# Gate, output projection, norm and first GEMM of the second block as one program by token tiles

## The chip, the cores and the metric

The kernel runs on one core of one Trainium2 chip. The metric is the device time of one execution in microseconds, as the median over runs. Engines are called as in the profile: PE (TensorE), DVE (VectorE), ACT (ScalarE), POOL (GpSimd) and SP (SyncE, which here only issues transfers).

## The reference, cut to what matters

Two transformer blocks follow each other on 1024 tokens of width 1024, all in float32. The piece around the change:

```python
        o_diff = rms_norm(o_diff, diff_subln_g[layer]) * (1.0 - lam_init)
        o_diff = o_diff.transpose(0, 2, 1, 3).reshape(B, T, DIFF_WIDTH) * jax.nn.silu(dz)
        ...
        o_nsa = o_nsa.transpose(0, 3, 1, 2, 4).reshape(B, T, NSA_WIDTH) * jax.nn.silu(nz)
        x = x + jnp.concatenate([o_diff, o_nsa], axis=-1) @ w_out[layer]
    return x
...
        h = rmsnorm(x, norm_mix_pre[i])
        proj = h @ w_in[i]
        z, xbc, dt_raw, q, k, v = jnp.split(proj, IN_OFFSETS, axis=-1)
```

The norm of `o_diff` is over each head's 128 columns, that of x over all 1024.

## The kernel before

The kernel is a row of stages, each a block of five engine programs that ends with a barrier and orders itself by semaphores that are written out by hand. Nothing schedules it: on each engine the order is that of the code. Tokens are tiled by 128 (`NT` = 8 tiles), the contraction by 128 (`KT` = 8 steps).

A product keeps float32 accuracy by splitting: ACT copies an operand into the rounded format fp32r (the high part), DVE subtracts it from the original (the low part), and PE adds up high x high, low x high and high x low, three matmuls for one. So each 128x512 tile of weights costs ACT a copy and DVE a subtraction, and so does each half of a transposed tile of activations.

Between the last attention stage of the first block ("di") and the windowed attention of the second ("w2") there were five stages:

- "mt", `transposed_stage` with the `prep` of line 1379. DVE squares and sums the heads of all eight tiles, ACT takes all roots at once, then DVE builds tile after tile: norm, gain `subln`, gate z (loaded back from DRAM by SP), the NSA half. PE transposes a tile in eight pieces of 128x128, ACT and DVE write its high and low part into `mT`.
- "o1", `gemm_stage` with two jobs of 512 columns. k is the outer loop, and all eight token tiles' banks are open; a ring of three weight tiles is split by ACT and DVE. DVE adds x (loaded into `xr`) in each bank at the end of a job; POOL issues the loads of x and the stores of x1.
- `end_part` (line 2990): SP clears all semaphores used so far.
- `params2_stage` (line 1430): small parameters and masks of the second block; ACT's Exp on `nA` waits for all of them.
- "n2", `norm_transposed` (line 1204): ACT squares all eight tiles of x1 with a sum along the row, one root, one reciprocal; then DVE scales a row and PE transposes it, into `h2T`.
- "g2", `gemm_stage` with four jobs: two of 512 columns of Q, one of K (each key column twice), one of 288 columns of V and dt. Q and K are column jobs (weights stationary, banks of 128 columns x 512 tokens), V is a row job. POOL builds the tables of the window attention meanwhile (`window2_tables`).

The last stage, `mix_mlp_stage` (line 2365), is written in another way, with class `Weights` (line 2195): every weight tile has a place of its own (`slot`) that is filled as soon as a named job has released it, and up to eight loads are on the way. Its output projection runs tile by tile: `mix_product(c, t)` adds the 24 matmuls of one token tile and one half of the columns into one bank, and the transpositions of a later tile stand between two products. Four banks hold products and four hold transpositions.

## Time and profile before

| | us |
|---|---|
| median of 3 runs | 3121.11 |
| lowest and highest | 3121.0, 3122.52 |
| the profiled execution's own time | 3118.35 |
| its span | 3116.6 |
| PE busy | 2692.8 |
| DVE busy | 1454.6 |
| ACT busy | 1022.3 |
| POOL busy | 236.0 |

The span runs from the first to the last instruction of the profiled execution; what lies between it and the execution's own time is its start and end. Busy times of engines overlap, so they don't add up to the span. The mean granted clock of PE is 0.923 of full speed (2.4 GHz); a stretch that shows 0.50 ran at the lower of its two levels.

### The profile page before, as it was taken

How to read it: one execution, taken by the hardware profiler on the slowest of the kernel's cores; microseconds unless marked ns; L12 is line 12 of the kernel's file. 1: busy time of each engine (PE TensorE's matmuls, PEld its weight loads, DVE VectorE, ACT ScalarE, POOL GpSimd, SP SyncE). 2: the span in 40 equal slices, each digit the busy share in tenths (PEclk: the TensorE clock that was granted, in tenths of full speed). 3: DMA queues.
4: the chain of work that ended last, by engine and by line, in shares of the span. 5: the costliest groups of instructions: out<-in, count | busy, mean ns of one | idle time of the engine just before them, and what ended most of it. 6: DMA issues, size and time to landing. Idle time of an engine off the chain costs nothing. (4 is left out here: it accounts for less than half of the span.)

```text
span 3116.6 us, 35479 instructions
## 1 busy us (share of the span) xinstructions
PE 2692.8 (86%) x13168; PEld 2186.9 (70%) x13168; DVE 1454.6 (47%) x3307; ACT 1022.3 (33%) x2250; POOL 236.0 (8%) x240
## 2 busy tenths in 40 slices
PE   3999966799966758498998998989869999999998
PEld 2888855677955646387666887567457888888877
DVE  3111157756788862313882212556776322322234
ACT  3112233344664410313882113245134212222132
POOL 1000002000020000200110000023600000000000
PEclk8999976698988969699999999979989999999999
DMA  2112210000000032110003112100044111111113
GB/s 88 49 48 76 65 56 1 1 1 1 1 1 1 1 138 78 39 48 19 23 24 114 48 64 82 54 1 1 1 172 146 41 55 48 48 48 48 51 48 139
DMA packets 102651, 153.10 MB, mean 49 GB/s; under 512 B 35024, under 2 KB 49488, under 8 KB 102480
## 3 DMA queue, kind: packets, MB, share of 16 engines
q1 hardware_dynamic: 95312, 125.67, 13.0%
q0 software_dynamic: 4864, 16.78, 1.4%
q10 hardware_dynamic: 2304, 8.39, 0.7%
q8 instruction: 105, 1.72, 0.2%
q14 instruction: 66, 0.54, 0.1%
HBM read 121.44 MB, written 29.36 MB: 48 GB/s over the span
## 5 line engine op out<-in xcount | busy, mean ns | idle before, releaser
L2280 PE MATMUL banks<-mhT,mmwhi 128*128 128x512 f32 x1024 | 316.2, 390 | 3.9 <-ACT qsq L2589 2.8
L2271 PE MATMUL banks<-mmwhi,fT 128*128 128x512 f32 x1024 | 315.8, 390 | 3.7 <-ACT qsq L2589 3.7
L381 PE MATMUL banks<-g1whi,hT 128*128 128x512 f32 (+1 forms) x1024 | 301.7, 378 | 5.7 <-DVE g1wlo L347 5.7
L2256 DVE TENSOR_TENSOR mmwlo<-mmwraw,mmwhi 128x512 fp32r<-128x512 f32 x144 | 97.2, 689 | 369.3 <-ACT mmwhi L2252 369.3
L2252 ACT ACTIVATE mmwhi<-mmwraw 128x512 fp32r<-128x512 f32 x144 | 89.3, 629 | 413.5 <-DMA mmwraw<-in_w_down 207.4
L2271 PEld LDWEIGHTS banks<-mmwhi,fT 128*128 128x128 f32 x1024 | 191.8, 188 | 45.3 <-ACT qsq L2589 5.5
L2280 PEld LDWEIGHTS banks<-mhT,mmwhi 128*128 128x128 f32 x1024 | 191.6, 188 | 45.5 <-ACT qsq L2589 4.1
L381 PEld LDWEIGHTS banks<-g1whi,hT 128*128 128x128 f32 x1024 | 189.2, 189 | 41.3 <-DVE g1wlo L347 6.1
L2271 PE MATMUL banks<-mmwlo,fT 128*128 128x512 f32 x512 | 199.3, 389 | 0.0
L2280 PE MATMUL banks<-mhT,mmwlo 128*128 128x512 f32 x512 | 199.3, 389 | 0.0
L381 PE MATMUL banks<-g1wlo,hT 128*128 128x512 f32 (+1 forms) x512 | 193.4, 378 | 0.0
L347 DVE TENSOR_TENSOR g1wlo<-g1raw,g1whi 128x512 fp32r<-128x512 f32 (+1 forms) x64 | 42.4, 662 | 261.2 <-ACT g1whi L324 261.1
L381 PE MATMUL banks<-h2T,g3whi 128*128 128x512 f32 x384 | 119.7, 393 | 7.5 <-DVE g3wlo L347 7.5
L381 PE MATMUL banks<-h2T,g2whi 128*128 128x512 f32 x384 | 119.8, 393 | 5.8 <-DVE g2wlo L347 5.8
L324 ACT ACTIVATE g1whi<-g1raw 128x512 fp32r<-128x512 f32 (+1 forms) x64 | 38.9, 607 | 251.4 <-PE banks L381 246.7
L2271 PEld LDWEIGHTS banks<-mmwlo,fT 128*128 128x128 f32 x512 | 96.1, 188 | 20.1
L2280 PEld LDWEIGHTS banks<-mhT,mmwlo 128*128 128x128 f32 x512 | 96.1, 188 | 19.9
L381 PEld LDWEIGHTS banks<-g1wlo,hT 128*128 128x128 f32 x512 | 96.5, 189 | 17.5
L347 DVE TENSOR_TENSOR g3wlo<-g3raw,g3whi 128x512 fp32r<-128x512 f32 x40 | 27.6, 692 | 169.8 <-ACT g3whi L324 169.6
L2104 ACT ACTIVATE sdE<-banks,vnA 128x128 f32<-128x128 f32 x256 | 69.9, 376 | 74.0 <-PE banks L2050 74.0
L1667 PE MATMUL banks<-w2pt,v 128*128 128x512 f32 x176 | 92.3, 609 | 0.0
L2089 DVE TENSOR_TENSOR sdE<-sdE,CBT 128x512 f32<-128x512 f32 x64 | 69.5, 1104 | 48.3 <-ACT sdE L2104 48.3
(451 smaller groups left out, 5788.3 us busy)
## 6 DMA issues: line engine op xcount, KB each, us to landing
mmwraw<-in_w_up SPq DMA_DIRECT2D x64, 256.0 KB, 2.7
mmwraw<-in_w_down SPq DMA_DIRECT2D x64, 256.0 KB, 2.6
g1raw<-in_w_in SPq DMA_DIRECT2D x56, 256.0 KB, 2.6
g3raw<-in_w_in SPq DMA_DIRECT2D x40, 256.0 KB, 2.6
qx<-x_scratch SPq DMA_DIRECT2D x16, 512.0 KB, 6.5
xt<-in_x SPq DMA_DIRECT2D x8, 512.0 KB, 6.5
z_scratch<-zst POOLq DMA_DIRECT2D x16, 256.0 KB, 2.6
cw<-in_cmp_w SPq DMA_DIRECT2D x2, 2048.0 KB, 9.3
```

Source lines behind the costliest of these rows:

```text
L324: nc.scalar.activation(whi[n % RING][:, w_slice(n)], raw[n % RAW][:, w_slice(n)], ACT.Copy).then_inc(hi_ready, 1)
L347: nc.vector.tensor_tensor(wlo[n % RING][:, w_slice(n)], raw[n % RAW][:, w_slice(n)], f32(whi[n % RING][:, w_slice(n)]), ALU.subtract).then ...
L381: last = nc.tensor.matmul(out, l, r, start=(k == 0 and i == 0), stop=(k == job.nk - 1 and i == 2))
L1667: nc.tensor.matmul(psum[6 + w % 2][:, :], v2[:, k, w % G // 2 * 2 * HD:(w % G // 2 + 1) * 2 * HD], pt[c % PT][:].rearrange("p h q -> p (h ...
L2089: nc.vector.tensor_tensor(E[u % 4][:], E[u % 4][:], CBT[:, c, g:g + 1, :].to_broadcast([P, 4, P]), ALU.mult).then_inc(g_ready, 1)
L2104: nc.scalar.activation(E[u % 4][:, i, :], psum[u % 4][:, i * P:(i + 1) * P], ACT.Exp, bias=V["nA"][:, d, c, 4 * q + i:4 * q + i + 1]).then ...
L2252: self.nc.scalar.activation(self.hi[n][:], self.raw[n][:], ACT.Copy).then_inc(self.hi_ready, 1)
L2256: self.nc.vector.tensor_tensor(self.lo[n][:], self.raw[n][:], f32(self.hi[n][:]), ALU.subtract)\
L2271: ins = self.nc.tensor.matmul(out, l, r[:], start=k == 0 and i == 0, stop=k == self.nk[j] - 1 and i == 2)
L2280: ins = self.nc.tensor.matmul(out, l[:, col], r, start=k == 0 and i == 0, stop=k == self.nk[j] - 1 and i == 2)
```

## The change

The five stages from the gate to the first GEMM become one block, `mix1_qkv_stage`. Class `Weights` moves up in the file and learns weight tiles of less than 512 columns and tiles that come in two loads. What is new or in another place:

- DVE's norm of the heads goes tile by tile: ACT squares a tile's 512 columns into the row buffer, DVE sums, ACT takes four roots per row, and one DVE operation per head multiplies norm and gate. The gain `subln` is multiplied into the z tile by POOL.
- The output projection runs tile by tile in two passes (first the left half of the columns for all tiles, then the right). The transpositions of tile t + 2 stand behind the product of tile t in the first pass. x1 overwrites `o_diff` and `o_nsa`.
- The norm of x1 is in two parts: ACT squares and sums the left half between the passes, the right half as it comes, and the root takes the left half's sum as its bias. Stores of x1 are issued by ACT in half tiles. The rows of tile t - 2 are transposed behind the product of tile t in the second pass, those of tiles 6 and 7 between the first products of V.
- V and dt come first of the second block's jobs, tile by tile, then Q in two jobs and K.
- The parameters of the second block are loaded and its masks built inside this block; the semaphores of the earlier stages are cleared by SP during the attention stage.
- K's low part, V and the tables get other places in memory.

```diff
+    old = list(used)
+    def clear_old(sp, o_done):
+        for s in old:
+            sp.sem_clear(s)
+    attention_stage(nc, sem, "di", mem, C, units, 2, psum2, psum, 41, 73, 81, store=clear_old)
...
+    first_slots = [153 + 4 * i for i in range(KT)]
+    second_slots = [4 * i for i in range(6)] + [41, 45]
+    for c in range(2):
+        w.job(NT, [(wo[k * P:(k + 1) * P, half_cols(c)], (first_slots if c == 0 else second_slots)[k], None)
+                   for k in range(KT)])
...
+    JV = w.job(NT, [(v_and_dt(k), first_slots[k], w.release(0, k)) for k in range(KT)], 256 + H2)
+    JQ = [w.job(8, [(s, second_slots[k], w.release(1, k)) if k < 7 else (s, first_slots[0], w.release(JV, 0))
+                    for k, s in enumerate(columns(C_Q))])]
...
+                if i >= XR:
+                    sp.wait_ge(mixed, i - XR + 1)
...
+            load_z(0)
+            load_z(1)
+            for n in w.steps(0):
+                w.load(sp, n)
+            sp.dma_start(C["gain"][:], a["norm_mix_pre_2"][0].partition_broadcast(P)).then_inc(g_in, 16)
+            for i in range(XR):
+                load_x(i)
+            for t in range(2, NT):
+                load_z(t)
+                w.load(sp, KT + t - 2)
+            w.load(sp, KT + 6)
+            w.load(sp, KT + 7)
+            for i in range(XR, NT):
...
+            for n in w.steps(JV):
+                w.load(sp, n)
+            for i in range(NT, 2 * NT):
+                load_x(i)
...
+            for j in (JQ[0], JQ[1], JK):
+                for n in w.steps(j):
+                    w.load(sp, n)
...
+            for t in range(NT):
+                pool.wait_ge(z_in[t % 2], 16 * (t // 2 + 1))
+                nc.gpsimd.tensor_tensor(zt[t % 2][:, 0:512].rearrange("p (h d) -> p h d", h=4),
+                                        zt[t % 2][:, 0:512].rearrange("p (h d) -> p h d", h=4),
+                                        C["subln"][:].unsqueeze(1).to_broadcast([P, 4, P]), ALU.mult).then_inc(zs, 1)
+            pool.wait_ge(zs, NT)
+            pool.wait_ge(mixed, 2 * NT)
+            pool.wait_ge(small_in, 16 * 10)
+            T["build"](pool, C["sink"][:])
+            pool.wait_ge(t2, 2 * NT)
...
+                if t >= 2:
+                    act.wait_ge(t1, 2 * (t - 1))
+                nc.scalar.activation(row[t % 2][:, 0:512], o_diff[:, t, :], ACT.Square).then_inc(o_sq, 1)
...
+            def norm_root(t):
+                act.wait_ge(mixed, NT + t + 1)
+                nc.scalar.activation(zj[t % 2], x1[1][:, t, :], ACT.Square, accum_out=st[:, t, 10:11]).then_inc(b_sq, 1)
+                act.wait_ge(b_sq, t + 1)
+                act.wait_ge(a_bias, t + 1)
+                nc.scalar.activation(st[:, t, 11:12], st[:, t, 10:11], ACT.Sqrt, scale=1.0 / DM, bias=st[:, t, 9:10])\
+                    .then_inc(x_root, 1)
+                store(1, t)
...
+            head_squares(0)
+            head_roots(0)
+            head_squares(1)
+            for n in range(2):
+                w.high(act, n)
+            high(0, t1, hi1)
+            for n in range(2, KT):
+                w.high(act, n)
+            head_roots(1)
+            for t in range(NT):
+                if t + 2 < NT:
+                    head_squares(t + 2)
+                if t >= 1:
+                    high(t, t1, hi1)
+                if t + 2 < NT:
+                    head_roots(t + 2)
+                w.high(act, KT + t)
...
+            for t in range(NT):
+                if t >= 2:
+                    act.wait_ge(b_sq, t - 1)
+                norm_root(t)
+                if t >= 2:
+                    high(t - 2, t2, hi2)
+                w.high(act, w.first[JV] + t)
+            for t in range(NT - 2, NT):
+                high(t, t2, hi2)
...
+            for t in range(NT):
+                if t < 7:
+                    w.high(act, w.first[JQ[0]] + t)
+                v_rows(t)
...
+            def rows(t):
+                dve.wait_ge(o_root, t + 1)
+                nc.vector.reciprocal(st[:, t, 4:8], st[:, t, 4:8]).then_inc(o_rec, 1)
+                dve.wait_ge(o_rec, t + 1)
+                dve.wait_ge(zs, t + 1)
+                for h in range(4):
+                    d = tile(h)
+                    nc.vector.scalar_tensor_tensor(out=row[t % 2][:, d], in0=o_diff[:, t, d], scalar=st[:, t, 4 + h:5 + h],
+                                                   in1=zt[t % 2][:, d], op0=ALU.mult, op1=ALU.mult).then_inc(r_done, 1)
+                nc.vector.tensor_tensor(row[t % 2][:, 512:1024], o_nsa[:, t, :], zt[t % 2][:, 512:1024], ALU.mult)\
+                    .then_inc(r_done, 1)
...
+            head_sums(0)
+            rows(0)
+            head_sums(1)
+            for n in range(2):
+                w.low(dve, n)
+            low(0, hi1, lo1)
+            rows(1)
+            for n in range(2, KT):
+                w.low(dve, n)
+            for t in range(NT):
+                if t + 2 < NT:
+                    head_sums(t + 2)
+                if t >= 1:
+                    low(t, hi1, lo1)
+                if t + 2 < NT:
+                    rows(t + 2)
+                w.low(dve, KT + t)
+                if t >= 1:
+                    mix(0, t - 1)
+            mix(0, NT - 1)
+            for t in range(NT):
+                mix(1, t)
+                bias(t)
+                if t >= 2:
+                    low(t - 2, hi2, lo2)
+                x_rows(t)
+                w.low(dve, w.first[JV] + t)
...
+            def mix_product(c, t):
+                if c == 0:
+                    pe.wait_ge(lo1, 2 * (t + 1))
+                if NT * c + t >= 4:
+                    pe.wait_ge(mixed, NT * c + t - 3)
+                for k in range(KT):
+                    if t == 0:
+                        pe.wait_ge(w.lo_ready, KT * c + k + 1)
+                    w.rows(c, k, hT, k, tile(t), psum[t % 4][:], t == NT - 1)
...
+            def v_product(t):
+                pe.wait_ge(lo2, 2 * (t + 1))
+                if t < 4:
+                    pe.wait_ge(mixed, NT + 5 + t)
...
+                    pe.wait_ge(v_done, t - 3)
+                for k in range(KT):
+                    if t == 0:
+                        pe.wait_ge(w.lo_ready, w.first[JV] + k + 1)
+                    w.rows(JV, k, hT, k, tile(t), psum[t % 4][:, 0:256 + H2], t == NT - 1)
...
+            t1_rows(0)
+            t1_rows(1)
+            for t in range(NT):
+                mix_product(0, t)
+                if t + 2 < NT:
+                    t1_rows(t + 2)
+            for t in range(NT):
+                mix_product(1, t)
+                if t >= 2:
+                    t2_rows(t - 2)
+            v_product(0)
+            v_product(1)
+            t2_rows(6)
+            v_product(2)
+            v_product(3)
+            t2_rows(7)
+            for t in range(4, NT):
+                v_product(t)
...
-    transposed_stage(nc, sem, "mt", C["ident"], DM, mT[0], mT[1], rowbuf, prep, psum, load=load_z, act_prep=act_prep)
...
-    gemm_stage(nc, sem, "o1", mem, 153, [out_job(0), out_job(1)], psum, pool_jobs=store_x1)
...
-            sp.wait_ge(x1_out, 16 * NT)
...
-    norm_transposed(nc, sem, "n2", mem, C, lambda t: x1[:, t, :], hT[0], hT[1], psum, 57, None, none)
...
-    gemm_stage(nc, sem, "g2", mem, 153,
...
-        end_part(nc, used)
```

`w.high(act, n)` is ACT's copy of weight tile n and `w.low(dve, n)` DVE's subtraction; `high` and `low` are the same for a transposed tile. `release(j, k)` is the point at which job j has used its weight tile k for the last time.

PE where the projection begins. Before, all transpositions ("mrow" is the row buffer) stand ahead, then a barrier (the branches), and the first matmuls take one weight tile through different token tiles:

```order
L209 MATMUL banks<-ident,mrow_11579 128x128 x8
L209 MATMUL banks<-ident,mrow_11578 128x128 x8
L209 MATMUL banks<-ident,mrow_11579 128x128 x8
L171 UNCONDITIONAL_BRANCH
L353 UNCONDITIONAL_BRANCH
L381 MATMUL banks<-o1whi_138_11883,mT_11574 128x512
L381 MATMUL banks<-o1whi_138_11883,mT_11575 128x512
L381 MATMUL banks<-o1wlo_141_11886,mT_11574 128x512
L381 MATMUL banks<-o1whi_138_11883,mT_11574 128x512
L381 MATMUL banks<-o1whi_138_11883,mT_11575 128x512
```

In the change, two tiles are transposed ("prow"), and then the first token tile goes through the weight tiles ("pjwhi", "pjwlo"):

```order
L1828 UNCONDITIONAL_BRANCH
L1833 MATMUL banks<-ident,prow_11760 128x128 x8
L1833 MATMUL banks<-ident,prow_11761 128x128 x8
L1317 MATMUL banks<-pjwhi_11712,h2T_11697 128x512
L1317 MATMUL banks<-pjwhi_11712,h2T_11698 128x512
L1317 MATMUL banks<-pjwlo_11711,h2T_11697 128x512
L1317 MATMUL banks<-pjwhi_11715,h2T_11697 128x512
L1317 MATMUL banks<-pjwhi_11715,h2T_11698 128x512
L1317 MATMUL banks<-pjwlo_11714,h2T_11697 128x512
L1317 MATMUL banks<-pjwhi_11718,h2T_11697 128x512
```

The transpositions of the later tiles have moved behind the products of earlier ones.

DVE for one tile of the gate. Before ("mT" is the transposed activation, two halves):

```order
L1393 TENSOR_TENSOR msq_11580<-o_diff_9879,mstat_11582 128x512
L1394 TENSOR_TENSOR msq_11580<-msq_11580,subln 128x512
L1396 TENSOR_TENSOR mrow_11579<-msq_11580,zt_11577 128x512
L1398 TENSOR_TENSOR mrow_11579<-o_nsa_3922,zt_11577 128x512
L1401 COPY mstat_11582<-mstat_11582 128x1
L186 TENSOR_TENSOR mT_11575<-banks,mT_11574 128x4x128 x2
```

In the change, for the first pass's fifth round ("pjwlo" is a weight tile's low part, L1752 the residual):

```order
L1727 TENSOR_REDUCE pstat_11765<-prow_11760 128x4
L1745 TENSOR_TENSOR h2T_11698<-banks,h2T_11697 128x4x128 x2
L1732 RECIPROCAL pstat_11765<-pstat_11765 128x4
L1737 SCALAR_TENSOR_TENSOR prow_11760<-o_diff_9879,pstat_11765,pz_11758 128x128 x4
L1739 TENSOR_TENSOR prow_11760<-o_nsa_3922,pz_11758 128x512
L1301 TENSOR_TENSOR pjwlo_11747<-pjwraw_11746,pjwhi_11748 128x512
L1752 TENSOR_TENSOR o_diff_9879<-banks,pxt_11762 128x512
```

The gain's product has left DVE, and a weight tile and a residual of the projection have come between two tiles' rows.

ACT where the second block's first products end. In the change the copies of the last two transposed tiles ("h2T", four halves) stand ahead of the first evacuation of V ("v", "dt_raw"), with the split of Q's first weight tile between them:

```order
L1637 DMA x_scratch<-o_nsa_3922 128x512
L1633 ACTIVATE h2T_11697<-banks 128x4x128 x2
L1296 ACTIVATE pjwhi_11733<-pjwraw_11731 128x288
L1633 ACTIVATE h2T_11697<-banks 128x4x128 x4
L1296 ACTIVATE pjwhi_11736<-pjwraw_11734 128x512
L1690 ACTIVATE v_129_11701<-banks 128x256
L1692 ACTIVATE dt_raw_11703<-banks 128x32
L1296 ACTIVATE pjwhi_11739<-pjwraw_11737 128x512
```

Before, V's evacuation was the last work of its stage, and no copy of an activation stood near it.

## Rows read from the trace of the kernel before

**Rows 1.** The page: busy time (share) x instructions; then a group of matmuls with its idle time.
```profile
PE 2692.8 (86%) x13168; PEld 2186.9 (70%) x13168; DVE 1454.6 (47%) x3307; ACT 1022.3 (33%) x2250; POOL 236.0 (8%) x240
...
L381 PE MATMUL banks<-h2T,g2whi 128*128 128x512 f32 x384 | 119.8, 393 | 5.8 <-DVE g2wlo L347 5.8
```

**Rows 2.** Stretches: us, busy us (instructions) of PE, PEld, DVE, ACT, POOL, granted clock, DMA share, GB/s.
```profile
1094.30:1144.60 50.30, 15.79 (x65) 12.59 (x65) 43.81 (x74) 12.08 (x20) 3.52 (x7) 0.54 0.30 98
1144.60:1149.30 4.70, 4.70 (x11) 3.73 (x12) 0.72 (x2) 0.98 (x2) 0.80 (x2) 0.50 0.99 371
1149.30:1234.20 84.90, 84.86 (x374) 69.88 (x373) 19.17 (x29) 8.22 (x13) 3.05 (x6) 1.00 0.23 83
1234.20:1302.30 68.10, 14.14 (x64) 11.51 (x64) 22.85 (x33) 22.99 (x38) 12.74 (x34) 0.55 0.26 67
1302.30:1306.30 4.00, 3.99 (x9) 3.14 (x10) 1.55 (x2) 0.63 (x1) 3.62 (x5) 0.50 0.65 190
1306.30:1434.70 128.40, 128.40 (x568) 106.31 (x567) 24.71 (x36) 23.54 (x38) 1.64 (x4) 1.00 0.18 43
1434.70:1460.30 25.60, 25.60 (x194) 25.35 (x192) 4.55 (x9) 6.00 (x19) 0.00 (x0) 1.00 0.08 19
```

**Rows 3.** Groups of instructions, 1094 to 1142 us: busy us, mean ns | idle before it, releaser.
```profile
L209 PE MATMUL banks<-ident,mrow 128*128 128x128 f32 x64 | 15.8, 428 | 29.3 <-DVE mstat L1401 29.3
...
L1384 DVE TENSOR_REDUCE mstat<-msq 128x4 f32<-128x512 f32 x8 | 5.5, 686 | 0.3
```

**Rows 4.** Timeline, 1252 to 1463 us: start us, length us, engine, line, operation [idle before, releaser].
```profile
1252.14 0.33 SPq L1453 DMA_DIRECT2D gain<-in_norm_mix_pre  x1
...
1263.23 0.23 ACT L1489 ACTIVATE nA<-nA 128x32 f32<-128x32 f32 x1 [9.80 <-DMA convb<-in_conv_b]
...
1278.05 3.67 PE L209 MATMUL banks<-ident,n2rb 128*128 128x128 f32 x16 [43.89 <-DVE n2rb L1227]
...
1462.03 1.06 ACT L1694 ACTIVATE w2qs<-q2T 64x1024 fp32r<-64x1024 f32 x1 [0.28 <-PEq L291]
```

**Rows 5.** Timeline of the last stage's start (the last row is a stretch, as in rows 2).
```profile
2274.62 0.32 SPq L2459 DMA_DIRECT2D qz<-z_scratch  x1
...
2277.80 1.22 DVE L2630 TENSOR_TENSOR y<-y,qz 128x1024 f32<-128x1024 f32 x1 [3.46 <-DMA qz<-z_scratch]
...
2296.78 1.97 PE L2772 MATMUL banks<-ident,y 128*128 128x128 f32 x8 [10.51 <-DVE y L2625]
2298.40 1.20 PE L2271 MATMUL banks<-mmwhi,mhT 128*128 128x512 f32 x2
...
2304.55 1.04 PE L2772 MATMUL banks<-ident,y 128*128 128x128 f32 x8
...
2317.23 1.04 PE L2772 MATMUL banks<-ident,y 128*128 128x128 f32 x8
...
2274.60:2298.40 23.80, 3.59 (x17) 3.20 (x17) 14.27 (x20) 12.11 (x22) 0.00 (x0) 0.52 0.92 338
```

**Rows 6.** Groups of instructions of the whole span, one engine each.
```profile
L1161 DVE SCALAR_TENSOR_TENSOR dix<-dix,dist,dix 128x512 f32<-128x512 f32 x4 | 3.0, 751 | 0.1
L1161 DVE SCALAR_TENSOR_TENSOR dix<-dix,dist,dix 128x128 f32<-128x128 f32 x4 | 1.4, 350 | 0.1
L324 ACT ACTIVATE o1whi<-o1raw 128x512 fp32r<-128x512 f32 x16 | 10.1, 632 | 68.9 <-PE banks L381 61.1 <-DMA o1raw<-in_w_out 7.8
L2926 ACT ACTIVATE v<-banks 128x256 f32<-128x256 f32 x8 | 3.0, 379 | 6.2 <-PE banks L381 6.2
L609 POOL TENSOR_TENSOR hntmp<-nq,hnrstd 128x512 f32<-128x512 f32 x8 | 10.1, 1258 | 69.7 <-DVE hnrstd L624 62.5 <-DVE hnst L632 7.2
```

**Rows 7.** Timeline, 1475 to 1483 us, POOL and DVE.
```profile
1475.39 2.35 POOL L1735 TENSOR_TENSOR w2qs<-q2T,w2qs 64x1024 fp32r<-64x1024 f32 x1 [167.15 <-ACT w2qs L1694]
1475.65 2.11 DVE L1767 TENSOR_TENSOR w2sk<-w2low,wnsink 128x4 f32<-128x4 f32 x1
...
1482.48 0.16 DVE L1767 TENSOR_TENSOR w2sk<-w2low,wnsink 128x4 f32<-128x4 f32 x1
```

More of the change, by code:

```diff
@@ L1233, in silu_store, with tile, half_cols @@
+def tile(t):
+    return slice(t * P, (t + 1) * P)
+def half_cols(c):
+    return slice(c * 512, (c + 1) * 512)
 def silu_store(nc, name, sem, stage, jobs_z, scratch, table_of):
@@ L1254, in silu_store, with first_block @@
     return take, pool_jobs
-def first_block(nc, sem, mem, a, C, S, big, x1_dram, scr_z):
+def first_block(nc, sem, mem, a, C, S, big, scr_z, used):
     psum = [big[:, 512 * i:512 * (i + 1)] for i in range(8)]
@@ L1356, in first_block @@
                               o_diff[:, t, h * P:(h + 1) * P], False))
-    attention_stage(nc, sem, "di", mem, C, units, 2, psum2, psum, 41, 73, 81)
-    mT = [mem.at("mT", 89 + 32 * i, [P, KT, SEQ], F32R) for i in range(2)]
-    zt = [mem.at("zt", 8 * i, [P, DM], F32) for i in range(2)]
-    rowbuf = [mem.at("mrow", 73 + 4 * i, [P, DM], F32) for i in range(2)]
-    sq = [mem.at("msq", 81 + 2 * i, [P, 4, P], F32) for i in range(2)]
-    stat = mem.at("mstat", 85, [P, 2, NT * 4], F32)
-    z_in = [sem(f"z_in{i}") for i in range(2)]
@@ L1417, in store_x1 @@
-    def store_x1(pool, act_out, dve_out, table):
-        for t in range(NT):
-            pool.dma_start(xr[:, t, :], x[t * P:(t + 1) * P, :]).then_inc(xr_in, 16)
-        for t in range(NT):
-            pool.wait_ge(dve_out, NT + t + 1)
-            pool.dma_start(x1_dram[t * P:(t + 1) * P, :], xr[:, t, :]).then_inc(x1_out, 16)
-    gemm_stage(nc, sem, "o1", mem, 153, [out_job(0), out_job(1)], psum, pool_jobs=store_x1)
-    S["x1_out"] = x1_out
-    return xr
-def params2_stage(nc, sem, mem, a, C, x1_out):
+    old = list(used)
@@ L1432, in params2_stage, with params2_layout @@
+def params2_layout(mem, C):
     mem.const_at = mem.kept
@@ L2284, in tile @@
-def tile(t):
-    return slice(t * P, (t + 1) * P)
-def half_cols(c):
-    return slice(c * 512, (c + 1) * 512)
 def attn_part_stage(nc, sem, mem, wo, ya, y_in, part_dram, psum, a_kb, w_kb, part_kb, part_out):
@@ L2868, in _, with second_block @@
                             w.rows(j, k, fT[k // 4], k % 4, tile(t), psum[t][:], t == NT - 1)
-def second_block(nc, sem, mem, a, C, S, big, x1, x1_dram, scr_z, scr_yT, part_dram, x2_dram, out, used):
+def second_block(nc, sem, mem, a, C, S, big, o_diff, o_nsa, x1_dram, scr_z, scr_yT, part_dram, x2_dram, out, used):
     psum = [big[:, 512 * i:512 * (i + 1)] for i in range(8)]
-    params2_stage(nc, sem, mem, a, C, S["x1_out"])
+    params2_layout(mem, C)
     hT = [mem.at("h2T", 89 + 32 * i, [P, KT, SEQ], F32R) for i in range(2)]
-    none = lambda eng, t: None
-    norm_transposed(nc, sem, "n2", mem, C, lambda t: x1[:, t, :], hT[0], hT[1], psum, 57, None, none)
@@ L2879, in second_block @@
     w = a["w_in_2"][0]
     qT = mem.at("q2T", 0, [P, ATT_HEADS // 2, SEQ], F32)
-    kT = [mem.at("k2T", 32 + 16 * i, [P, ATT_KV, SEQ], F32R) for i in range(2)]
-    v2 = mem.at("v2", 64, [P, NT, ATT_KV * HD], F32)
+    k_hi = mem.at("k2T", 32, [P, ATT_KV, SEQ], F32R)
+    v2 = mem.at("v2", 48, [P, NT, ATT_KV * HD], F32)
+    k_lo = mem.at("k2T", 56, [P, ATT_KV, SEQ], F32R)
     dt_raw = mem.at("dt_raw", 88, [P, NT, 2 * SSM_HEADS], F32)
-    T = window2_tables(nc, sem, mem, 183, 183.75, 171)
-    qscale = T["qscale"]
@@ L3017, in build @@
         params1_stage(nc, sem, mem, a, C)
-        x1 = first_block(nc, sem, mem, a, C, S, big, x1_dram, scr_z)
-        end_part(nc, used)
-        second_block(nc, sem, mem, a, C, S, big, x1, x1_dram, scr_z, scr_yT, part_dram, x2_dram, out, used)
+        o_diff, o_nsa = first_block(nc, sem, mem, a, C, S, big, scr_z, used)
+        second_block(nc, sem, mem, a, C, S, big, o_diff, o_nsa, x1_dram, scr_z, scr_yT, part_dram, x2_dram, out, used)
 _INS = ["x", "norm_g", "w_in", "diff_q_norm_g", "diff_k_norm_g", "diff_lambda_q1", "diff_lambda_k1",
```

503 lines of the change are left out of this document (314 added, 189 removed).

## The prediction

> **What bounds the kernel now.** I read the page first: TensorE (PE) is busy 86% of the span, VectorE (DVE) 47%, ScalarE (ACT) 33% [rows 1]. So PE is the bound and the changed part is worth what PE waits in it, not what its other engines do. The table of stretches splits that part by PE's state [rows 2]. The last attention value is evacuated at 1094.3 us; then come 50.3 us in which PE is busy 15.8 (64 transpositions at a granted clock of 0.54), the output projection (4.7 us at half clock, 84.9 at full), 68.1 us in which PE is busy 14.1, and the first GEMM of the second block (4.0 us at half clock, 128.4 at full for Q and K, 25.6 for V and dt). From 1094.3 to 1460.3 that is 366.0 us.
>
> The two holes have plain causes. In the first, DVE is busy 43.8 of 50.3 us: it squares and sums all eight tiles before ACT takes the roots, then builds the rows tile by tile, with PE waiting 29.3 us for it [rows 2, 3]. In the second, small loads and semaphore clearing come first: no engine computes from 1235 to 1252.1, the Exp on nA waits 9.8 us for the last parameter, then ACT squares eight tiles before the first row exists; PE waits 43.9 us in one piece [rows 4]. Inside the first GEMM of the second block PE waits for nothing but the first weights, 5.8 us [rows 1], and its products fill the projection's stretch just as tightly [rows 2]. So there is room to win only in the holes and the two warm-ups.
>
> **The sum, part by part.** The new program uses the pattern that the kernel has already in its last stage (gate, transposition, output projection by token tiles), so most prices can be read there.
>
> *Products.* Their number is unchanged. Q and K are 576 matmuls in 132.4 us; half of the 4.0 us at half clock is lost, so 130.4 us is the full-clock cost, 0.226 each. The projection's 384 give 89.6 - 2.4 = 87.2 us. V is 25.6 [rows 2]. Together 243.2 us. The order changes from k outside to tile outside, so 24 matmuls in a row add into one bank. In the last stage a tile done that way takes 5.44 us (2298.40 to 2304.55 is 6.15 with the warm-up, and the next two repeat every 6.34 with transpositions) [rows 5]: 24 x 0.227, no charge.
>
> *Transpositions.* Of 16 groups of eight, 14 now stand between products. A group with its neighbours' switching costs 6.34 - 5.44 = 0.9 us at full clock [rows 5], against 1.97 at half clock in the holes [rows 5]. 14 x 0.9 = 12.6 us on the path.
>
> *The start.* From 1094.6: z of tile 0 lands after 3.2 us (2274.62 to 2277.80) [rows 5]; the new GpSimd (POOL) product of z with subln takes 1.26 like a 128x512 product in the first block [rows 6], to 4.5. Square, sum (0.6 + 0.69), a table load and the root of tile 0 are ready before that. DVE's row is four products of 128x128 at 0.35 and one of 128x512 at 0.69, as long as a sum [rows 3, 6], to 6.6; transposition 2.0, to 8.6. Tile 1 comes next, but its root stands on ACT behind the splitting of six weight tiles, and these behind z0, z1 and the weights before them on one queue: 3 MB. At the 338 GB/s of the last stage's start [rows 5] that is 9 us and some 3 of latency, so the root is there at about 13, the row at 15.2, and the first product 1.6 us after its transposition begins [rows 5]: 17.2 us after 1094.3 with the stage's change. The lower bound is 13 (weights early). The upper is 23.8, which the last stage took from its first load to its first product [rows 5]; there one more load of 512 KB stands before the weights, and the whole z tile is gated on DVE ahead of the second row. So I take 17.2. Warm-up: the last stage lost 0.7 us in its first tile, the projection 2.4; I take 1.2.
>
> *First pass.* PE needs 6.34 per tile. DVE has, per tile, a sum, two low parts, a weight's low part and the residual, which are five operations of 128x512 at 0.69 or a little less, and a row of 2.1 + 0.2: 5.6 [rows 3, 6]. As a chain from the end of one transposition (ACT's square 0.6 first) that is 6.2 to 6.3, just inside PE's period; PE needs the low parts 3.7 us later than they come. Charge 0.
>
> *Second pass and V.* DVE's chain after tile 7 is residual 0.7, ACT's square, root and store issue, its two copies, DVE's low parts, two scaled rows of 0.75 each [rows 6], then the low part of V's last weight tile: about 6.2 us after the product's end. V's first tile reaches that weight at 0.9 + 7 x 0.4 = 3.7. Wait 2.5. POOL begins its table work then, see below; 3.0 with it. Second wait: ACT copies hT for tiles 6 and 7 before it evacuates any V tile, and tile 7's transposition stands behind V tile 3. V tile 4 needs bank 0 back, which comes 1.2 us of copies, 0.63 of a weight and the evacuation (0.38 and a smaller one) after the transposition, counted with the copy that overlaps it: 2.1 [rows 6]. Bounds 0 and 8 for the two waits together. Q and K start without a wait: their weights are loaded under V.
>
> *Small loads, constants, masks, x1 stores.* Under 200 us of products; on SyncE's queue the parameters stand before Q's weight loads, which are due some 30 us later, and ACT issues 16 stores between its squares. Charge 0. If that cover were gone, it is the 18 us before 1252.1 and the 11 after it [rows 4]. The block change itself (semaphores cleared) moves under 140 us of attention.
>
> *Tail.* K ends the program now instead of V: the last bank's copy 0.6 and low part 0.69 against V's shorter evacuation; but that runs behind today, and the next stage starts 1.7 us after PE ends at 1460.3 [rows 4]. Equal.
>
> Sum: 17.2 + 1.2 + 243.2 + 12.6 + 5.1 = 279.3 against 366.0: 86.7 us less. The profiled execution's own time is 3118.35 (span 3116.6 and 1.75 around it), so 3031.7 by it. The median of the runs is 3121.11, 2.8 above; I forecast the median of runs: **3034**.
>
> **GpSimd beside VectorE.** The rows show a price that the sum leaves out. While POOL multiplies for 2.35 us, a DVE product of 128x4 takes 2.11 us and ends with it; alone it takes 0.16 [rows 7]. The new pass has a POOL product of 1.26 per tile, and DVE's row products and weight low parts read two SBUF operands. Eight times 1.26 is 10 us if all of it fell on PE's path. By the chain it falls at 1.7 to 3.0 us after the transposition, under the low parts, which read one operand from PSUM (whether these wait too, no row shows), and PE has 3.7 us of slack; so I charge 0.5 at V only.
> The Trainium skill (SBUF — State Buffer, section "SBUF: two separate sides") says why: the two engines share one port pair, taken as a lock for a whole instruction. By that rule the sum would be between +0 and +10 us; this trace agrees that the wait is the whole rest of POOL's instruction.
>
> **Rivals.**
> 1. *DVE's chain paces the first pass.* For: 6.2 to 6.3 of 6.34 us leaves nothing, and locks of up to 1.26 come on top. Against: in the last stage DVE gates a whole tile (1.22 [rows 5]), scales it, and does the same low parts and residual, and PE keeps 6.34. With 7.5 per tile over 7 to 12 tiles: +8 to +14, 3042 to 3048. It needs PE's slack of 3.7 to be used up first.
> 2. *Loads hold the start.* As in the last stage, 23.8 instead of 17.2: 3041.
> 3. *Half clock through both passes, slower than before.* In the first hole PE worked half of the time, in bursts of transpositions, and the granted clock stayed at its lower level (1.2 of 2.4 GHz): mean 0.54 there, 0.55 in the second [rows 2]. If the tile program made PE pause in every tile, by a late row or a late bank, the clock could stay there: 384 products and 14 groups cost 87 + 13 more, plus the pauses, 3134 and up. It decides from about 14 of 16 tiles at the lower level, since the gain is 86.7 and a tile costs 6.3. Against it: 6.34 us per tile in the last stage is the full clock.
> The Trainium skill (TensorE: Matmul & The Clock Gate, section "HAM oscillation — how this bites in real kernels") tells of a kernel that fell back in every K tile because it waited for a load there; here by that rule only tiles with a wait would pay, and the last stage's rows show none.
> 4. *The change doesn't bring its overlap*, because a queue order serialises one pass (SyncE holds the x tiles behind z tile 7 and 16 loads of V): one hole of about 40 us comes back, 3075.
>
> **How the numbers follow.** Forecast 0.72 (3025 to 3041, with starts of 13 to 20 and waits of 0 to 8); rival 1 0.12; rival 2 0.10; rival 4 0.04; rival 3 0.02. The range of 3024 to 3048 holds the forecast and rivals 1 and 2 and leaves less than 2 in 10 outside. What a measurement can tell from no change here is about 0.2%, 6 us. Faster 0.975, within 0.015 (a mix of rivals 3 and 4), slower 0.01.
>
> **What would show it.** Right: about 17 us from the end of the attention to the first product; transposition groups every 6.3 us in both passes at clock 1.00; one wait of 2 to 3 us at V's first tile for a weight's low part, one near V's fifth tile for ACT; no wait at Q. Wrong: a wait at each product of the first pass (rival 1), loads as releasers before 1112 (rival 2), matmuls of over 0.6 us after the first tile (rival 3), or a hole of tens of us between the passes (rival 4).

## The result and the profile after

| | before | changed |
|---|---|---|
| median of the runs, us | 3121.06 (4 runs) | 3031.32 (4 runs) |
| lowest and highest | 3119.87, 3122.52 | 3026.34, 3039.78 |
| the profiled execution's own time | 3118.35 | 3032.81 |
| its span | 3116.6 | 3031.1 |

The changed kernel takes 0.9715 of the time before (95% interval 0.9692 to 0.9738): 89.7 us less by the medians, 85.5 by the profiled executions. Forecast were 3034 and 86.7 less by the profiled execution. A second comparison of the same two kernels gave 3030.49 and 0.9717 (0.9700 to 0.9735).

The page, as in [rows 1] (the second row is the group with V's first tile in it):

```profile
PE 2680.7 (88%) x13168; PEld 2179.8 (72%) x13168; DVE 1444.6 (48%) x3325; ACT 1024.3 (34%) x2286; POOL 247.0 (8%) x236
...
L1317 PE MATMUL banks<-pjwhi,h2T 128*128 128x512 f32 (+1 forms) x384 | 108.2, 368 | 4.7 <-DVE pjwlo L1301 2.5
```

PE is busy 12 us less and the span is 85.5 shorter. In the stretches between the end of the attention and the end of the GEMM alone PE was busy 277.5 of 366.0 us [rows 2] and is now busy 263.0 of 283.2: its idle time fell by 68.3, and the same matmuls take 14.5 less, since fewer run at the lower clock. The stretches, with the columns of [rows 2]: the start, the first tile, the two passes, V and dt, then Q and K.

```profile
1092.90:1111.95 19.05, 3.59 (x17) 3.19 (x17) 10.29 (x21) 8.95 (x16) 4.84 (x3) 0.63 0.79 281
1111.95:1119.00 7.05, 7.05 (x28) 5.71 (x27) 6.58 (x14) 2.31 (x5) 4.34 (x2) 0.79 0.29 103
1119.00:1211.90 92.90, 92.53 (x457) 77.36 (x456) 57.88 (x117) 33.95 (x82) 6.56 (x4) 1.00 0.50 146
1211.90:1245.40 33.50, 29.13 (x212) 28.69 (x211) 12.48 (x19) 11.86 (x31) 20.64 (x41) 0.95 0.12 40
1245.40:1376.10 130.70, 130.70 (x578) 107.91 (x576) 21.20 (x31) 21.66 (x36) 0.30 (x1) 1.00 0.12 32
```

The first hole of [rows 2] is now 19.05 us long, and in the place of the second stands nothing, since V follows the second pass in the same microsecond. In the 92.9 us of the passes PE waits once, for 0.4 us. All waits of PE in the stage (waited for: us in total, times, longest):

```profile
PE banks L1833 <- DVE prow L1739: 15.9, 2, 9.9
PE banks L1317 <- DVE pjwlo L1301: 2.5, 1, 2.5
PE banks L1317 <- ACT dt_raw L1692: 1.8, 1, 1.8
PE banks L1317 <- DVE h2T L1745: 0.4, 1, 0.4
```

The start in the timeline (start us, length us, engine, line, operation [idle before, releaser]):

```profile
1093.15 0.82 SPq L1544 DMA_DIRECT2D pz<-z_scratch  x2
...
1098.32 2.48 POOL L1587 TENSOR_TENSOR pz<-pz,subln 128x512 f32<-128x512 f32 x2 [157.12 <-DMA pz<-z_scratch]
...
1099.68 2.05 DVE L1737 SCALAR_TENSOR_TENSOR prow<-o_diff,pstat,pz 128x128 f32<-128x128 f32 x4 [4.06 <-POOL pz L1587]
...
1104.89 3.21 ACT L1296 ACTIVATE pjwhi<-pjwraw 128x512 fp32r<-128x512 f32 x6
1108.00 0.28 ACT L1627 ACTIVATE pstat<-pstat,eps 128x4 f32<-128x4 f32 x1
...
1108.53 1.14 DVE L1737 SCALAR_TENSOR_TENSOR prow<-o_diff,pstat,pz 128x128 f32<-128x128 f32 x4
...
1110.33 1.97 PE L1833 MATMUL banks<-ident,prow 128*128 128x128 f32 x8 [5.97 <-DVE prow L1739]
```

The loads of z were issued from 1093.15 on, and GpSimd began its product for tile 0 at 1098.32. The four row products of tile 0 took 2.05 us beside GpSimd's work on tile 1, those of tile 1 took 1.14. ScalarE copied six weight tiles (3.21 us) before tile 1's root at 1108.00, and PE waited 5.97 for the row that hangs on that root.

**How far the runs lie apart.** The changed kernel's four runs lie 13.4 us apart, those of before 2.7 here and up to 11.5 in later comparisons. To compare stages I therefore use three marks of each trace: the end of the last attention value's evacuation, the first product of the projection, and the end of the GEMM's last matmul (K's in the changed kernel, V's before). A time with a plus sign is counted from the first mark. The stage between the first and the last mark took 283.25 us in the changed kernel (366.0 before), and 281.69 in the second profile.

### The profile page after: what moved, and what is told of

The parts are those of the page before. It is cut to its first block and busy times, and to the rows that moved or that the text cites. A ratio compares the mean times of both kernels' runs of the same rounds, so it can differ in the third digit from the quotient of the medians.

```text
span 3031.1 us, 35487 instructions
## 1 busy us (share of the span) xinstructions
PE 2680.7 (88%) x13168; PEld 2179.8 (72%) x13168; DVE 1444.6 (48%) x3325; ACT 1024.3 (34%) x2286; POOL 247.0 (8%) x236
## 5 line engine op out<-in xcount | busy, mean ns | idle before, releaser
L1326 PE MATMUL banks<-h2T,pjwhi 128*128 128x512 f32 x384 | 118.3, 389 | 0.0
L1317 PE MATMUL banks<-pjwhi,h2T 128*128 128x512 f32 (+1 forms) x384 | 108.2, 368 | 4.7 <-DVE pjwlo L1301 2.5
```

The costliest lines, as they stand in the source:

```text
L1317: ins = self.nc.tensor.matmul(out, l, r[:, c], start=k == 0 and i == 0, stop=k == self.nk[j] - 1 and i == 2)
L1326: ins = self.nc.tensor.matmul(out, l[:, col], r, start=k == 0 and i == 0, stop=k == self.nk[j] - 1 and i == 2)
```

## The experiments

**The same kernel again.**

> The changed kernel as it is, in five rounds beside the kernel before, to see how far its runs lie apart. Its four runs so far lie between 3026.3 and 3039.8, those of before between 3119.9 and 3122.5. If the spread belongs to the new stage, the stretch from the end of the attention to the last matmul of K (283.2 us in the first profile) moves by several us from one profile to the next; if it belongs to the rest of the kernel, that stretch stays within 1 us and other stretches move. Median 3031, ratio 0.9715.

Median 3030.49 (3025.4 to 3036.6). The stage moved by 1.6 us, 1.5 of it in V (33.46 and 31.97 from V's first product to Q's first), a little more than the 1 us that I had set as the sign. What moved more is far away, in the diagonal part of the scan (the stage that writes `sdE`): 143.9 us in the first profile, 147.6 in this one, 140.8 in the order experiment below. The stretch in this profile, and in that of the order experiment:

```profile
1974.80:2122.40 147.60, 141.35 (x827) 118.27 (x827) 80.69 (x95) 70.23 (x256) 48.32 (x24) 0.85 0.00 1
```

```profile
1977.30:2118.10 140.80, 133.85 (x827) 112.06 (x827) 81.29 (x95) 69.81 (x256) 48.36 (x24) 0.90 0.00 1
```

The same 827 matmuls under a granted clock of 0.85 and of 0.90: 6.8 us between two executions in a stage that the change does not touch. So small edits are read from the stage's own marks, and only their sum from the medians.

**One part of the change alone, in the kernel before.** Clearing of semaphores, small loads and masks:

```diff
-    attention_stage(nc, sem, "di", mem, C, units, 2, psum2, psum, 41, 73, 81)
+    attention_stage(nc, sem, "di", mem, C, units, 2, psum2, psum, 41, 73, 81, store=clear_old)
...
-    gemm_stage(nc, sem, "o1", mem, 153, [out_job(0), out_job(1)], psum, pool_jobs=store_x1)
+    gemm_stage(nc, sem, "o1", mem, 153, [out_job(0), out_job(1)], psum, pool_jobs=store_x1, load_more=small_loads)
...
-        end_part(nc, used)
```

> The kernel before with one part of the change alone: the semaphores are cleared by SyncE during the attention, the eleven small loads are issued and the masks built under the output projection, and what is left between projection and norm is the Exp and four small VectorE operations. My theory: this part is worth what no engine computes in between, 18 us, and most of the 11 us up to the first squares of the norm, less a barrier and the wait for the last stores that stay: 22 to 28 us, so 3093 to 3099. The other 58 to 63 us of the change need the program by token tiles. The rival (most of the gain is the tidying between the stages): 50 us or more, 3070 or less.

Median 3094.54, ratio 0.9921 (0.9906 to 0.9936): 24 us less than the kernel before in the same comparison (median 3118.93), inside the 22 to 28 that I expected. The stage's marks say 17.5 (348.5 against 366.0), which is less than that: the rest lies outside the marks, where in the profiles the attention ended 4.9 us earlier and what follows took 3.5 less. The hole before the norm went from 68.1 to 50.4:

```profile
1231.00:1239.00 8.00, 0.00 (x0) 0.00 (x0) 0.00 (x0) 0.00 (x0) 0.00 (x0) 0.62 0.79 317
1239.00:1242.50 3.50, 0.00 (x0) 0.00 (x0) 1.64 (x4) 1.51 (x2) 0.00 (x0) 0.50 0.01 2
1242.50:1254.00 11.50, 0.00 (x0) 0.00 (x0) 0.41 (x2) 10.77 (x18) 0.00 (x0) 0.50 0.00 1
1254.00:1273.00 19.00, 13.16 (x64) 10.97 (x64) 18.02 (x23) 8.88 (x16) 0.00 (x0) 0.65 0.00 0
```

The 8 us without a computing engine that are left are stores of x1 (317 GB/s) behind the projection's end. They are in the kernel before too, where the DMA share is 1.02 up to 1239 us, 0.73 in the next 4 us and 0 behind them; I had put all 18 us down to clearing and small loads. So tidying is worth a fifth of the gain, and the rival that it is most of it falls.

**The overlap of the first pass taken back.** All tiles of the gate are transposed first:

```diff
-            t1_rows(0)
-            t1_rows(1)
+            for t in range(NT):
+                t1_rows(t)
             for t in range(NT):
                 mix_product(0, t)
-                if t + 2 < NT:
-                    t1_rows(t + 2)
...
                 w.low(dve, KT + t)
-                if t >= 1:
-                    mix(0, t - 1)
-            mix(0, NT - 1)
+            for t in range(NT):
+                mix(0, t)
```

> The changed kernel with all eight tiles of the gate transposed ahead of the first product; everything else stays. My theory: VectorE needs some 5 us per tile there (sum 0.67, row 2.0 to 2.9, low parts 1.3, a weight's low part 0.6), so the first product comes 6 x 5 = 30 us later, 6 x 0.9 us of groups no longer stand between products, and warm-up costs about 1 more: +25, so 3056 (3051 to 3061), with a granted clock near 0.5 through the transpositions. The rival (the overlap is worth little, since the time of the first hole went by the cheaper row and the missing barrier): less than +8, under 3040.

Median 3054.95, ratio 0.9793 (0.9776 to 0.9809), stage 307.52: +24.3. The first product comes 47.85 us after the attention's end, nearly the 50.3 of before. The last three of the six transpositions behind the first two, and the stretch:

```profile
1129.22 1.97 PE L1832 MATMUL banks<-ident,prow 128*128 128x128 f32 x8 [2.29 <-DVE prow L1739]
1133.47 1.97 PE L1832 MATMUL banks<-ident,prow 128*128 128x128 f32 x8 [2.28 <-DVE prow L1739]
1137.73 1.97 PE L1832 MATMUL banks<-ident,prow 128*128 128x128 f32 x8 [2.29 <-DVE prow L1739]
...
1110.30:1139.35 29.05, 12.10 (x52) 9.70 (x51) 28.42 (x64) 14.76 (x31) 14.37 (x6) 0.50 0.46 152
```

VectorE is busy 28.42 of 29.05 us and gives a row every 4.25 us (5 expected; the first of the six took 7.5). PE waits 2.3 us for each of the last five, at half clock. So the cheaper row and the missing barrier alone are worth 2.5 us of the first hole; the overlap takes it from 47.85 to 19.08.

**The overlap of the second pass taken back.** Squares and sums stay in the pass; only rows and transpositions go behind it:

```diff
             for t in range(NT):
                 mix_product(1, t)
-                if t >= 2:
-                    t2_rows(t - 2)
+            for t in range(NT):
+                t2_rows(t)
```

> The changed kernel with the rows of x1 transposed behind the whole second pass instead of between its products; squares and sums stay where they are. My theory: per tile 2 x 0.75 for the scaled row and 1.3 for the low parts on VectorE, 3.2 us with the small ones, eight tiles 26 us and 2.5 ahead of them, a warm-up of 1.5; the 7 us of groups inside the products and the two waits of 2.5 and 1.8 us in V go: +18, so 3049 (3044 to 3054). The rival (half clock follows into V and Q): V at half clock adds 20 us more, 3065 and up.

Median 3044.76, ratio 0.9765 (0.9747 to 0.9783), stage 297.39: +14.1. From the last product (1207.43) to V's first (1232.46) it takes 25.0 us; a row came every 2.72 us, not 3.2. V's first 4 us ran at a granted clock of 0.52 and the other 23 at 1.00, so it had a warm-up, and the rival (half clock through V and Q) falls. With the experiment on the small loads this splits the second hole of before: 68.1 to 50.4 by tidying, and 50.4 to 25.0 by what this variant keeps, which are x1's stores, the sums of squares and the weight splitting under the pass and one barrier less. The last 25.0 go by transposing between products, which is worth 14.1 net, as the groups and the two waits of V then stand in the products. Together the three experiments account for 17.5 + 24.3 + 14.1 = 55.9 of the stage's 82.8 us; the other 26.9 were not taken back by themselves, so how they divide is not shown.

**GpSimd beside VectorE.** More products of 128x256 into a spare place behind each product with subln, two and then five per tile:

```diff
+                for _ in range(5):
+                    p_spare.link(nc.gpsimd.tensor_tensor(spare[:], C["subln"][:].unsqueeze(1).to_broadcast([P, 2, P]),
+                                                         C["subln"][:].unsqueeze(1).to_broadcast([P, 2, P]), ALU.mult))
```

> The changed kernel with two more GpSimd products of 128x256 into a spare place behind each product of z with subln, so GpSimd's work beside the first pass is about doubled (16 more instructions of some 0.6 to 0.75 us). My theory: VectorE's operations that read two SBUF operands wait for the rest of a GpSimd instruction (its four row products took 2.05 us beside one and 1.14 without), but PE has slack of some 3.7 us per tile: the groups of transpositions stay 6.34 to 6.36 us apart from the third on, the first product comes at most 1 us later, and the stage from the first transposition to the last matmul (272 to 273 us) grows by 0 to 2. The rival (VectorE's chain is just inside PE's period, so each lock is paid): 0.7 to 1.3 us more per tile over six tiles, +5 to +8.

> The same with five more GpSimd products per tile, so GpSimd works some 5 of 6.3 us. My theory: each of the six SBUF operations that VectorE has per tile waits for most of a GpSimd instruction, 6 x 0.4 to 0.7, which makes a tile's chain 8.5 to 10 us; PE pauses 2 to 3.5 us in each tile of the first pass, and the first pass grows by 12 to 21. It also tries what I called half clock through a pass: with such pauses, do the matmuls stay at 0.39 us or go to 0.63, and does the granted clock of the first pass fall to 0.5 (then +35 and more) or stay near 1? I expect it to stay over 0.8. If VectorE does not wait for GpSimd at all, nothing moves (+0 to +1).

With two, the passes took 100.20 us from the first product to V (99.97 without), so my reading holds there; the start took 2.2 us more, where I had allowed 1. With five the start took 2.5 more and the passes 104.60: +4.6, not 12 to 21. (The single runs took 3031.76 and 3038.55.) VectorE's groups from 1125 to 1160 us, first of the changed kernel, then with five:

```profile
L1737 DVE SCALAR_TENSOR_TENSOR prow<-o_diff,pstat,pz 128x128 f32<-128x128 f32 x16 | 7.7, 541 | 0.1
L1745 DVE TENSOR_TENSOR h2T<-banks,h2T 128x512 fp32r<-128x512 f32 x11 | 7.1, 678 | 0.4 <-ACT h2T L1633 0.4
L1752 DVE TENSOR_TENSOR o_diff<-banks,pxt 128x512 f32<-128x512 f32 x6 | 4.1, 685 | 7.2 <-PE banks L1317 5.0 <-DMA pxt<-in_x 2.1
L1301 DVE TENSOR_TENSOR pjwlo<-pjwraw,pjwhi 128x512 fp32r<-128x512 f32 x6 | 4.1, 680 | 0.0
```

```profile
L1743 DVE SCALAR_TENSOR_TENSOR prow<-o_diff,pstat,pz 128x128 f32<-128x128 f32 x20 | 12.1, 664 | 0.2
L1751 DVE TENSOR_TENSOR h2T<-banks,h2T 128x512 fp32r<-128x512 f32 x12 | 7.6, 675 | 0.0
L1301 DVE TENSOR_TENSOR pjwlo<-pjwraw,pjwhi 128x512 fp32r<-128x512 f32 x6 | 5.3, 888 | 0.0
L1758 DVE TENSOR_TENSOR o_diff<-banks,pxt 128x512 f32<-128x512 f32 x6 | 4.1, 680 | 1.0 <-PE banks L1317 1.0
```

What reads two operands from SBUF grows (the row products from 350 ns alone to 541 and 664, the weights' low part from 680 to 888); what reads one from PSUM does not (678 and 675, 685 and 680). That was open in the prediction. VectorE's idle time before the residual, 7.2 us in these 35, is the slack that it had; with five it is 1.0, and PE pays: three of its groups of transpositions then stand 6.6 to 7.4 us apart instead of 6.35. The stretch shows that the clock stayed up:

```profile
1123.00:1160.00 37.00, 34.02 (x170) 27.95 (x171) 35.54 (x61) 12.27 (x27) 21.21 (x24) 1.00 0.42 136
```

PE paused 1.7 us (just ahead of this stretch) and 1.3 at this pass's beginning and 0.8 and 0.5 in its middle, all under a granted clock of 1.00. So such pauses did not bring half clock through the pass; longer ones in a pass weren't tried.

**One product of GpSimd later.**

```diff
+                if t == 1:
+                    pool.wait_ge(r_done, 5)
                 pool.wait_ge(z_in[t % 2], 16 * (t // 2 + 1))
```

> The changed kernel with one wait more: GpSimd's product for tile 1 starts when VectorE has written the row of tile 0. My theory: the four row products of tile 0 take 1.14 instead of 2.05 us, and everything behind them up to the first product of the projection comes 0.9 us earlier (17.6 to 18.4 us after the end of the attention instead of 19.1). If they are slow for another reason, they stay at 2.05 and nothing moves.

```profile
1100.27 1.14 DVE L1739 SCALAR_TENSOR_TENSOR prow<-o_diff,pstat,pz 128x128 f32<-128x128 f32 x4 [4.10 <-POOL pz L1589]
1101.32 0.68 DVE L1741 TENSOR_TENSOR prow<-o_nsa,pz 128x512 f32<-128x512 f32 x1
...
1102.52 1.98 DVE L1301 TENSOR_TENSOR pjwlo<-pjwraw,pjwhi 128x512 fp32r<-128x512 f32 x2
```

1.14 instead of 2.05, and the first product at +18.20 instead of +19.08. The lost time did not vanish: the two low parts of weights now take 1.98 instead of 1.28, but nothing waits for them. The stage as a whole shows nothing of it (283.77), since V took 34.87 us in this execution.

**Tile 1's roots first.**

```diff
+            head_roots(1)
             high(0, t1, hi1)
             for n in range(2, KT):
                 w.high(act, n)
-            head_roots(1)
```

> The changed kernel with tile 1's roots on ScalarE ahead of the copies of tile 0's transposition and of the six weight tiles. My theory: the root that came at 1108.0 comes at about 1103; the row is then bound by VectorE, which is free at 1105.7; the second transposition starts at 1107.8 instead of 1110.3 and the first product at 1109.4 instead of 1112.0: -2.5 us. The rival (the loads hold the start): the weights' copies are late themselves, and the first product moves by less than 0.5 us.

The root came at 1103.4, the second transposition at 1108.04, the first product at +16.14 instead of +19.08: -2.9. The loads did not hold it. Stage 280.48.

**The two waits in V.**

```diff
             for t in range(NT):
+                w.high(act, w.first[JV] + t)
                 norm_root(t)
                 if t >= 2:
                     high(t - 2, t2, hi2)
-                w.high(act, w.first[JV] + t)
...
+            v_rows(0)
+            high(6, t2, hi2)
+            v_rows(1)
+            v_rows(2)
+            v_rows(3)
+            high(7, t2, hi2)
```

(On VectorE `w.low` moves ahead of the residual in the same way.)

> The changed kernel with the two waits in V taken away by order alone: ScalarE and VectorE split V's weight tile t ahead of the norm of tile t instead of behind it, and ScalarE evacuates V's tiles 0 to 3 before it copies tile 7's transposition and splits Q's weights. My theory: the wait of 2.5 us at V's first tile and that of 1.85 at its fifth go, and with them the short fall of the granted clock behind them (matmuls of 0.44 us instead of 0.29 for about 3 us, in some executions), so from V's first product to Q's first it takes 27.5 to 28.5 us instead of 32.0 to 34.9, and the median falls by 4 to 7, to 3024 to 3027. A rival (the waits are moved, not removed: Q's first weight or its banks come late instead): Q's start waits 2 us or more and less than 2 us are won.

From V's first product to Q's it takes 27.11 us and PE waits for nothing, so the waits are gone and not moved. They had cost more than they last. In the eight profiled executions that have both waits, V took 31.97 to 34.87 us, in steps of about 1.5. The slowest, of the experiment with one product of GpSimd later:

```profile
1216.00:1220.00 4.00, 2.89 (x12) 2.89 (x13) 1.06 (x2) 0.00 (x0) 3.48 (x6) 0.58 0.00 0
1232.00:1236.00 4.00, 3.81 (x21) 3.84 (x22) 2.98 (x5) 3.53 (x11) 3.50 (x6) 0.71 0.02 4
1236.00:1240.00 4.00, 4.00 (x29) 4.00 (x28) 1.71 (x2) 1.10 (x3) 3.65 (x4) 0.86 0.00 0
```

Behind the wait of 2.5 us (in five of the eight) and that of 1.85 (in two) the granted clock fell, for 3 us or more. The median moved to 3028.25 only (3021.91 to 3037.4), where I had expected 3024 to 3027: two of its four runs were above 3033, and its profile has the scan's diagonal part at 147.6. The time of the runs alone would have hidden this edit.

**z of tiles 0 and 1 during the attention.** SyncE loads them behind the clearing, into 8 KB of each partition that are free there; tiles 2 and 3 then need no wait.

```diff
+        for i in range(2):
+            sp.dma_start(S["z_early"][i][:], scr_z[tile(i), :]).then_inc(S["z_early_in"][i], 16)
...
-            load_z(0)
-            load_z(1)
             for n in w.steps(0):
                 w.load(sp, n)
```

> The changed kernel with z of tiles 0 and 1 loaded during the attention, into a place of their own; z of tiles 2 and 3 no longer wait. My theory: at the start VectorE waits for z (4.0 us idle), not for ScalarE's root, so tile 0's row is ready at about 4.6 us after the attention's end instead of 9.5, the weights arrive 2 us earlier, and the first product comes 4.5 to 5.5 us earlier, at +13.5 to +14.6 instead of +19.1. The rival (the weights' loads set the start; z hides behind them): the first product moves by less than 2.5 us.

Tile 0's row was ready at +4.6 us (9.5 before) and the first product at +14.14: -4.9, as expected. Stage 278.35. The single run, 3032.98, shows nothing of it, again with 147.6 in the scan.

**All four edits, and two more.**

> Early z, tile 1's roots first, GpSimd's product of tile 1 behind tile 0's row, and the two waits in V taken away, all in one. The sum of my parts: the first product at +11.5 to +13 after the attention's end instead of +19.1 (the start is then a chain over VectorE and the weights, in which the parts overlap), and V 4.5 to 6.5 us shorter: 11 to 13 us less than the changed kernel, a median of 3017 to 3021. If the earlier start only makes PE wait for tile 2's row behind the first product, 3 us of it come back.

Median 3017.5, ratio 0.9678 (0.9664 to 0.9693); first product at +11.77, stage 271.25. PE now waited 0.93 us for tile 2's row and 1.29 for tile 1's low part. The last version moves the work behind these two waits:

```diff
             for n in w.steps(0):
+                if n == 4:
+                    load_z(2)
                 w.load(sp, n)
+            load_z(3)
...
-                if t >= 1:
-                    high(t, t1, hi1)
+                if t != 1:
+                    high(max(t, 1), t1, hi1)
```

> The version with all four edits, and two more: z of tiles 2 and 3 is loaded among and right behind the first eight weight tiles instead of behind the gain and three tiles of x, and the copy and low part of tile 1's transposition stand ahead of tile 2's row instead of behind a weight tile whose load comes late. With all four edits PE waited 0.93 us for tile 2's row and 1.29 for tile 1's low part. My theory: both waits go and the stage from the attention's end to the last matmul falls from 271.3 to 269 or 269.5; the median of the runs falls by about 2, to 3015 to 3016, which the scatter of the runs may hide. A rival (the weights come later by the z loads between them): PE waits inside the first product instead, and the stage stays at 271 or more.

Stage 269.23, median 3014.99, ratio 0.9673 (0.9652 to 0.9694). The start became 1.05 us longer (first product at +12.82): GpSimd's product for tile 2 now comes so early that it stands beside tile 1's row products, which take 2.21 us instead of 1.14. The passes became 3.1 shorter (98.54 against 101.61), and the rival (PE waits inside the first product) did not come. In the whole stage PE waits only for the rows of tiles 0 and 1:

```profile
PE banks L1852 <- DVE prow L1758: 9.6, 2, 5.0
```

Both versions beat the changed kernel, 13 and 15.5 us below its 3030.49; between the two the medians can't tell, the stage's marks can (2.0 us).

## Why the prediction was right

The forecast was the right case, and its time is 2.7 us above the median. It was not as exact as that. By the marks, the stage took 283.25 us, where the sum says 279.3: 4.0 too little. Two things outside the stage made up for it, and that is luck. In the profiled executions 2.75 us (85.5 - 82.75) were won there: the attention ended 1.4 us earlier and what follows took 1.3 less. And I took the median to be 2.8 above the profiled execution, as before, while it lies 1.5 below it. What follows is shared by both kernels and scatters by more than that. The attention now carries the clearing; it ended between 1089.4 and 1093.5 us in the thirteen profiles that have it and at 1094.3 in the one that hasn't. One profile is too few to tell whether the clearing does that.

- *The start, 17.2.* Measured 19.05. This is the term that was furthest off: z was to land after 3.2 us, as in the last stage [rows 5], and GpSimd got it after 5.2. Here two z tiles are issued within 0.8 us with the weights right behind them; that they share the transfer is my reading and wasn't tried by itself. Then the four row products took 2.05, since GpSimd worked on tile 1 meanwhile; I had the price [rows 7] and placed it at V only. For tile 1 the prediction had the right place (the root behind six weights, shown by moving it) and the wrong reason: the loads were not the bound, since the six copies ran back to back. They began only at 1104.89, behind the copies of tile 0's transposition, which stand ahead of them in ScalarE's order. So z and tile 0's row reached the first product by that way, and taking z early won the whole 4.9 us.
- *Warm-up, products, transpositions: 1.2 + 87.2 + 12 x 0.9 = 99.2 up to V.* Measured 99.97. Groups came every 6.34 to 6.36 us at clock 1.00 from the third tile on, as in the last stage. The first tile took 6.93 against 5.44, a warm-up of 1.5, and the second waited 0.4 for its low part.
- *V: 25.6 + 2 x 0.9 + 5.1 = 32.5.* Measured 33.46. The waits were 2.5 and 1.85 against 3.0 and 2.1, in the places named, for the low part and for ScalarE. The fall of the clock behind the first of them, 1.5 us here and 0 to 3 in other executions, was missing from the sum.
- *Q and K, 130.4; tail 1.7.* Measured 130.74 and 1.7; no wait at Q.
- *Small loads, masks, stores: 0.* No wait of PE names them, so they were hidden. But what their place was worth in the kernel before was 17.5 us, not the 29 that I set against them; 8 of the difference were the stores of x1.
- *Rival 1* (VectorE paces the pass) did not come: it had 1.3 us of slack per tile (7.2 us in 35), where the prediction left it next to nothing, and twice GpSimd's work changed nothing in the passes; with five more products per tile it does come, +4.6. *Rival 2* (loads hold the start) came in part, by z and not by the weights. *Rival 3*: no sign, even with pauses up to 1.7 us. *Rival 4*: no hole.

The rule of the Trainium skill that I weighed (SBUF — State Buffer, section "SBUF: two separate sides") names, apart from VectorE's 2-port perf modes, only its operations with two SBUF inputs. The traces agree: the row products went from 350 ns to 541 and 664, and those with an operand in PSUM did not change. On the clock (TensorE: Matmul & The Clock Gate, section "HAM oscillation — how this bites in real kernels") the case described there, a fall in every tile, did not arise; what was seen is a short fall behind a single wait of 2.5 us, in five executions of eight.

## What to carry to other kernels

Between stages that each end with a barrier, look at what PE does in the gaps: here two holes were 118 us long, and PE was busy for 30 of them. A program by tiles has no second hole and a first of 19 us, with the same matmuls. Of the second hole a quarter was tidying, over a third work that could stand under the product, and the rest the transpositions, of which 14 us were won in the end. Once the holes are closed, price the remaining waits with the clock that they may cost, and prove edits of a few us by marks around the stage, since a stage far away can move the total by 7 us.

## What was not expected

- One stage of the kernel, untouched, took 140.8, 143.9 or 147.6 us with clock 0.90, 0.88 or 0.85 in different executions.
- GpSimd waits as VectorE does: its product of 128x512 takes 1.26 us alone and took 5.44 beside VectorE's work at 1109.59 us, six low parts of weights in a row among it.
- A wait of 1.85 or 2.5 us on PE was followed by 3 us or more at the lower clock in some executions and not in others; none of the shorter pauses in the first pass was.
